# A gate panel ahead of the wait at two stage borders, and the split of the mixed sum in the last step of the last branch

## The reference, cut to what matters

```python
def _merge(att, conv, dn, gz, w_br, w_out):
    gates = jax.nn.sigmoid(gz)
    m = (gates[..., :D_MODEL] * (att @ w_br[0])
         + gates[..., D_MODEL:2 * D_MODEL] * (conv @ w_br[1])
         + gates[..., 2 * D_MODEL:] * (dn @ w_br[2]))
    return m @ w_out

def _token_mixer(u, uc, ...):
    pl = _split_cols(u @ w_in + b_in)
    pc = _split_cols(uc @ w_in + b_in)
    ...
    att_l = _attention_blocked(ql, k_all, v_all)
    conv_l = _short_conv(pl, sc_conv)
    dn_l, dn_c = _dn_bidirectional(...)
    out_l = _merge(att_l, conv_l, _dn_output(dn_l, pl[7], dn_norm_g), pl[12], w_br, w_out)
```

## Time and profile before

| | us |
|---|---|
| timed runs, median (three) | 3375.95 (3371.08 to 3377.99) |
| profiled execution | 3370.39 |
| its span | 3368.6 |
| TensorE matmul busy | 3188.0 (95%) |
| VectorE busy | 1731.9 (51%) |
| ScalarE busy | 1409.3 (42%) |
| DMA queue of the weights, share of 16 engines | 31.0% |
| panels' matmuls (line 1598) on the chain that ended last | 67% |

### The profile page before, as it was taken

How to read it: one execution, slowest core, us unless ns; L and a number is a source line. 1 busy time by engine, 2 the same in 40 slices (tenths; PEclk the granted TensorE clock), 3 DMA queues, 4 the chain that set the end, 5 groups by cost and what they waited for, 6 DMA issues and landing times.

```text
span 3368.6 us, 51444 instructions
## 1 busy us (share of the span) xinstructions
PE 3188.0 (95%) x18766; PEld 2650.5 (79%) x18766; DVE 1731.9 (51%) x3150; ACT 1409.3 (42%) x2197; POOL 131.5 (4%) x126
## 2 busy tenths in 40 slices
PE   4999999999989899999999999999899998899898
PEld 2777768888868578877788868787788888699898
DVE  2333357777743833434333343333678775756555
ACT  3222255565534632224322242223655654653544
POOL 0000001010100000000000000000000000000000
PEclk7999999999999999999999999999899999999999
DMA  6534431111122033222432243444211113144454
GB/s 234 175 127 151 153 113 45 50 50 44 54 66 88 14 115 130 99 87 95 168 100 94 94 144 137 162 133 153 73 48 51 61 45 115 60 142 164 152 183 146
DMA packets 101116, 363.43 MB, mean 108 GB/s; under 512 B 11136, under 2 KB 12672, under 8 KB 100864
## 3 DMA queue, kind: packets, MB, share of 16 engines
q1 hardware_dynamic: 98240, 353.02, 31.0%
q10 hardware_dynamic: 2752, 8.72, 0.8%
HBM read 360.58 MB, written 1.11 MB: 107 GB/s over the span
## 4 chain that ended last, share of the span: by engine, by line
PE 84%; DVE 7%; ACT 4%; issue 3%; DMA 1%; POOL 0%; SPq 0%; DVEq 0%; POOLq 0%; ACTq 0%
PE bank L1598 67%; PE bank L1847 3%; PE bank L1845 2%; DVE wlo L989 2%; PE bank L1623 2%; ACT whi L480 1%; PE bank L1898 1%; ACT scr L910 1%; PE bank L1906 1%; DVE h L1056 1%; PE bank L1916 1%; PE bank L1918 1%; PE bank L2051 1%; PE bank L2074 1%; ACT gc_row L893 1%
## 5 line engine op out<-in xcount | busy, mean ns | idle before, releaser
L1598 PE MATMUL bank<-uh,whi 128*128 128x512 f32 (+1 forms) x3008 | 1117.2, 371 | 49.6 <-ACTq L868 17.0
L1598 PE MATMUL bank<-ul,whi 128*128 128x512 f32 (+1 forms) x3008 | 1084.3, 360 | 0.0
L1598 PE MATMUL bank<-uh,wlo 128*128 128x512 f32 (+1 forms) x3008 | 1081.8, 360 | 0.5 <-DVE scr L1346 0.3
L480 ACT ACTIVATE whi<-raw 128x1024 fp32r<-128x1024 f32 x520 | 548.1, 1055 | 1223.1 <-PE bank L1598 1222.7
L989 DVE TENSOR_TENSOR wlo<-raw,whi 128x1024 fp32r<-128x1024 f32 x520 | 642.0, 1235 | 799.1 <-ACT whi L480 797.7
L1598 PEld LDWEIGHTS bank<-uh,whi 128*128 128x128 f32 x3008 | 577.7, 192 | 155.9 <-issue 60.4
L1598 PEld LDWEIGHTS bank<-uh,wlo 128*128 128x128 f32 x3008 | 576.7, 192 | 82.0 <-DVE scr L1346 1.8
L1598 PEld LDWEIGHTS bank<-ul,whi 128*128 128x128 f32 x3008 | 578.4, 192 | 69.9 <-issue 2.2
L1598 PE MATMUL bank<-bh,whi 128*128 128x512 f32 (+1 forms) x1088 | 387.9, 357 | 1.1 <-DVE h L1056 0.8
L1598 PE MATMUL bank<-bl,whi 128*128 128x512 f32 (+1 forms) x1088 | 384.5, 353 | 0.0
L1598 PE MATMUL bank<-bh,wlo 128*128 128x512 f32 (+1 forms) x1088 | 384.4, 353 | 0.0
(11 more groups left out here) (232 smaller groups left out, 3034.3 us busy)
## 6 DMA issues: line engine op xcount, KB each, us to landing
raw<-stream SPq DMA_DIRECT2D x520, 512.0 KB, 3.3
ada_raw<-stream SPq DMA_DIRECT2D x132, 512.0 KB, 5.1
gc_row<-gc_rows ACTq DMA_DIRECT2D x16, 512.0 KB, 3.7
m<-stream SPq DMA_DIRECT2D x8, 512.0 KB, 11.4
scr<-stream SPq DMA_DIRECT2D x4, 512.0 KB, 13.0
h<-h_in SPq DMA_DIRECT2D x1, 2048.0 KB, 17.3
cst<-consts SPq DMA_DIRECT2D x1, 1298.0 KB, 5.6
out<-m SPq DMA_DIRECT2D x8, 128.0 KB, 1.8
```

The lines of the kernel that those rows point to most:

```text
L480: act.activation(whi[:, j, :], raw[:, j, :], ACT.Copy).then_inc(hi_ready, 1)
L1598: last = mm(bank[j][:, c0:T], w(t, a), x[:, t, c0:T], start=n == 0, stop=n == 3 * kts - 1)
```

## The change

Three edits, in both layers:

1. **Attention to branch 1.** The first gate panel of branch 1 is moved into the attention stage: 6 of its 24 matmuls stand before the last `pv`, 18 behind it. `pair_done[0]` is now raised when the sixth tile's low part is done, and the wait for the attention output (`att_low`) stands before panel 1.
2. **Conv to branch 2.** The wait for conv's output stands before panel 1 of branch 2, not before panel 0.
3. **Branch 2 to output.** In the last step of branch 2, VectorE does 7 of the 8 subtractions of the mixed sum (`m_low`) before it waits for the last panel; ScalarE's copies have waits of their own: tiles 0 to 5 for the last panel but one, tiles 6 and 7 for their sums.

TensorE's branch loops start at 1 for all branches; block 0 is written out.

```diff
             def project_out(l):            # ScalarE
-                act.wait_ge(panel_done, 4 * B0)
-                have(act, pair_done[1], G0)
+                act.wait_ge(panel_done, 4 * B0 - 1)
+                have(act, pair_done[1], G0 - 1)
                 for t in range(KT):
+                    if t >= KT - 2:
+                        have(act, pair_done[t % 2], G0)
                     act.activation(uh[:, t, c0:T], m3[:, t, c0:T], ACT.Copy).then_inc(C["mh_ready"], 1)
...
+            def m_low(l, t):               # VectorE
+                c0 = CTX if l == DEPTH - 1 else 0
+                dve.wait_ge(C["mh_ready"], 8 * l + t + 1)
+                dve.tensor_tensor(ul[:, t, c0:T], m3[:, t, c0:T], uh[:, t, c0:T].bitcast(f32), ALU.subtract).then_inc(C["mx_ready"], 1)
...
                         split(B + 1, 2 * k)
+                        if last and k:
+                            for t in range(KT - 1):
+                                m_low(l, t)
                         dve.wait_ge(panel_done, 4 * B + 2 * k + 2)
...
+                        if j == 6:         # VectorE, out_low in attention
+                            dve.wait_ge(A["att_low"], 8 * l + 7)
+                            dve.sem_inc(pair_done[0], 2)
...
-                for k in range(2):
-                    dve.sem_inc(pair_done[k], 2)
+                dve.sem_inc(pair_done[1], 2)
...
-                for t in range(KT):
-                    dve.wait_ge(C["mh_ready"], 8 * l + t + 1)
-                    dve.tensor_tensor(ul[:, t, c0:T], m3[:, t, c0:T], ...)
+                m_low(l, KT - 1)
...
+                else:                      # TensorE, branch
+                    for j in range(4):
+                        if j == 1:
+                            for s, n in ready:
+                                have(pe, s, n)
+                        if (r, j) != (1, 0):
+                            pair_free(G0, j)
+                            panel(B0, j, *((uh, ul) if j % 2 == 0 else (bh, bl)), c0)
-                with pe.Fori(1 if r == 0 else 0, 4) as i:
+                with pe.Fori(1, 4) as i:
...
+                    if n == N:             # TensorE, attention
+                        pair_free(G1, 0)
+                        panel(B1, 0, uh, ul, c0, hi=6)
                     if n:
                         pv(n - 1)
                     if n < N:
                         turn(n)
+                panel(B1, 0, uh, ul, c0, lo=6)
...
-                branch(l, 1, [(pair_done[0], P[("q", l)][1] + 2), (pair_done[1], P[("q", l)][1] + 2)])
+                branch(l, 1, [(A["att_low"], 8 * l + 7)])
```

More of the change, by code:

```diff
@@ L1394, in branch, with step @@
                 g0, rides = P[("rides", l, "br")] if r == 1 else (0, 0)
-                def step(i):
+                def step(i, last=False):
                     B = B0 + i
@@ L1426, in branch @@
                         step(0)
-                    with steps.loop(1 if r == 0 else 0, 4, 0 if r == 0 else 2) as i:
+                    with steps.loop(1 if r == 0 else 0, 3 if r == 2 else 4, 0 if r == 0 else 2) as i:
                         step(i)
+                    if r == 2:
+                        step(3, True)
                 for k in range(2):
@@ L1552, in project_out @@
                 c0 = CTX if l == DEPTH - 1 else 0
-                for t in range(KT):
-                    dve.wait_ge(C["mh_ready"], 8 * l + t + 1)
-                    dve.tensor_tensor(ul[:, t, c0:T], m3[:, t, c0:T], uh[:, t, c0:T].bitcast(f32), ALU.subtract).then_inc(C["mx_ready"], 1)
+                m_low(l, KT - 1)
                 gates(l, 1)
@@ L1969, in branch @@
                 g0, rides = P[("rides", l, "br")] if r == 1 else (0, 0)
-                for s, n in ready:
-                    have(pe, s, n)
+                if r == 0:
+                    for s, n in ready:
+                        have(pe, s, n)
                 if rides:
@@ L1974, in branch @@
                         for j in range(4):
-                            pair_free(G0 + i, j)
-                            panel(B0 + i, j, *((uh, ul) if j % 2 == 0 else (bh, bl)), c0)
+                            if (i, j) == (0, 1):
+                                for s, n in ready:
+                                    have(pe, s, n)
+                            if (i, j) != (0, 0):
+                                pair_free(G0 + i, j)
+                                panel(B0 + i, j, *((uh, ul) if j % 2 == 0 else (bh, bl)), c0)
                             if j % 2 == 0:
@@ L1991, in branch @@
                             qk_swap(10 * l + j // 2, kT[:, j // 2, :])
-                with pe.Fori(1 if r == 0 else 0, 4) as i:
+                else:
+                    for j in range(4):
+                        if j == 1:
+                            for s, n in ready:
+                                have(pe, s, n)
+                        if (r, j) != (1, 0):
+                            pair_free(G0, j)
+                            panel(B0, j, *((uh, ul) if j % 2 == 0 else (bh, bl)), c0)
+                with pe.Fori(1, 4) as i:
                     for j in range(4):
@@ L2076, in pv @@
                     last.then_inc(A["s_pv"], 1)
+                B1, G1 = P[("br", l, 1)]
                 scores(0)
```

## The result

The changed kernel takes 3354.39 us, the median of six runs (3353.69 to 3357.12), against 3374.17 us for the kernel before, six runs as well. The ratio is 0.9944 (95% interval 0.9933 to 0.9955): faster by 0.56%, 15 to 23 us. The profiled execution has a span of 3352.2 us against 3368.6, 16.4 us less. Forecast were 15.6 us. Between the medians it is 19.8 us: the profiled execution of the kernel before (3370.39 us) was shorter than all six of its timed runs, so the traces show a smaller gain than the medians.

What follows compares the result with a forecast made beforehand. TensorE was taken to bound nearly everything, so removing its idle pays. Conv 12.0, attention 4.6 and output 0.3 - 1.3 sum to 15.6 us: 3375.95 - 15.6 = 3360.4 us, range 3351 to 3369.

Steps and rivals of the forecast that it cites:

- What bounds the kernel: Whole kernel: TensorE has 84% of the span, so an edit pays by the idle time it takes out of TensorE.
- Conv to branch 2: Wait moved behind the gate panel: panel 1 starts 6.7 us sooner in layer 0, 5.3 in layer 1, both 12.0 us.
- Attention to branch 1: Gate matmuls around the last pv fill both idle times: 2.4 us in layer 0, 2.2 in layer 1, both 4.6 us.
- Rivals C and D: C: gate panel only moves the wait, gain 0 to 6 us, chance 0.12. D: written-out blocks make it slower, 0.04.
- Branch 2 to output: No copy runs under the last panel, only the order behind it changes: layer 0 gains 0.3 us, layer 1 loses 1.3.
- rival B: Branch 2's end: the mixed sum really is split under the last panel; gain 24.6 us, 3351.4 us; chance 0.04.
- The forecast wait of some 2 us at tile 7: First output panel, both layers: TensorE stands some 2 us before tile 7, which is last in a longer line.
- 0.3 - 1.3: Second output panel's start after branch 2: 0.3 us gained in layer 0, 1.3 us lost in layer 1.
- The sum: All borders: 12.0 + 4.6 + 0.3 - 1.3 = 15.6 us, from the median 3375.95 to 3360.4 us.
- The clock: Output stage: full speed behind the new idles; slow starts of 1.5 us (layer 0) and 2.4 (layer 1) kept for the range.

Runs made afterwards that it cites:

- the kernel kept warm through the wait: Kernel before, with 18 (layer 0) or 30 (layer 1) matmuls of no use put into the wait behind conv: ratio 0.9993.
- split under the panel: Changed kernel, with ScalarE copying tiles 0 to 6 before slot 3's whi copy and VectorE subtracting tile 7 before the last wlo split: 3348.19 us.

## Why the prediction held, and where it did not

- **What bounds the kernel.** Held: only idle time of TensorE, and its slow matmuls behind it, moved.
- **Conv to branch 2.** Held, 12.3 us for 12.0, and no wait took the place of the old one in layer 0. In layer 1 the two idles were 0.3 and 0.8 us for 0.4 and 1.3. That part of this sum is the slow start was read from the spacing of the matmuls; the kernel kept warm through the wait shows it by itself, 3.8 us. These are distances in traces; edit 2 alone gained 8.9 us between medians, 6 to 13 by its interval.
- **Attention to branch 1.** Held, 4.8 us for 4.6, with both parts of the mechanism: the six before `pv` are worth 0.8 and 0.7 us, and bank 0 was free in time. Timed alone, edit 1 gained 1.1 us.
- **Rivals C and D.** No step was late, and written-out code costs nothing within 0.1%.
- **Branch 2 to output.** The order of the work held. ScalarE's order kept the split from running under the last panel (rival B did not happen, and the kernel that moves ScalarE's copies shows that the order alone was the reason). In layer 0 tile 7 decides, and the mark came 0.7 us earlier for 0.3; in layer 1 0.9 us later for 1.3, and that passed through to the stage's last product (28.62 us behind branch 2's last matmul for 27.71), as forecast. The forecast wait of some 2 us at tile 7 came only where the panel ran at full speed (1.56 us with edit 3 alone); in the changed kernel it was 0.17 us in layer 0.
- **The value of edit 3.** This is the term that failed: "0.3 - 1.3", 1.0 us lost. Beside edits 1 and 2, on one chip, edit 3 gained 3.8 us. The term was worked out against rows in which layer 1's output panel ran at full speed after 2.83 us of idle. Of six kernels without edit 3, all with 2.83 us of idle there, two had full speed behind it (before, and the one with block 0 written out: 6.3 us), and four did not (7.8 to 8.7 us), among them edits 1 and 2. In layer 0 the same six have the mark anywhere from 9.85 to 12.38 us. With edit 3 it is at 10.5 and 7.2 us in all four traces that have the change's order on ScalarE and VectorE, whether the panel starts fast or slowly. So edit 3 gains where the border would have had a long slow start, and loses 0.7 and 0.9 us where it would have had none. Of the 3.8 us the borders explain 2.4; the rest is open.
- **The sum.** It came out near by some luck. The forecast has 16.6 us for edits 1 and 2 and a loss of 1.0 for edit 3. Between medians, edits 1 and 2 gave 13.3 and 14.5 us in two comparisons, and edit 3 another 3.8, so an optimistic and a pessimistic term cancel in part (the first within its interval). Nor do the edits add up: alone they gave 1.1, 8.9 and 0.2 us, 10.2 in sum, against 18.3 and 19.8 for all three. Slow starts at the idles that a single edit leaves account for part of this in the traces; the rest stays open.
- **The clock.** I took full speed behind the new idles, with the slow starts in the range. In the changed kernel it was slow in layer 0 (first matmul 0.76 us) and from the ninth matmul on in layer 1, and it cost next to nothing, since the wait at tile 7 became shorter by as much (0.17 us for 1.56). The slow start was priced about right (1.4 us here for 1.5) and put in the wrong place: what mattered was which of the old ones would go. The 1.39 us of the earlier trace rows, which I took for a short idle followed by a low clock, did not stand alone: TensorE had stood 1.92 and 0.62 us in the six microseconds before, waiting for loads. The Trainium skill says ("TensorE: Matmul & The Clock Gate", section "A second HAM failure mode: psum-queue depth-cycling") that frequent short idles between groups of matmuls make the clock swing between its levels. The rows agree with it only in part: idles of 2.5 and 2.0 us were followed by slow matmuls in the changed kernel, and by full speed up to tile 7 with edit 3 alone. The 1.68 us at attention were followed by full speed in the kernel before (first matmul 0.47 us), but not with block 0 written out (0.77 us).

## What to carry to other kernels

To move work under a panel it is not enough to loosen a wait: follow the engine's own order upwards from the moved instruction, and look whether something ahead of it waits for that very panel. Where work on the busiest engine stands behind a wait that it does not need, move it ahead of the wait: it pays twice, for the idle and for the slow matmuls after it. And don't take a stretch behind an idle of 2 to 4 us from one trace as its price; the same idle was followed by either clock level in neighbouring kernels, and runs of one kernel differ by several microseconds.

## What the runs showed of the hardware that was not expected

- The same idle is followed by either clock level. 2.83 us before layer 1's output panel: granted clock 1.00 over seven microseconds in the kernel before, 0.53 with edits 1 and 2. 3.66 us before layer 0's: full speed with edit 2 alone, slow matmuls in the other five kernels without edit 3.
- Whether the kernel or the execution decides is open. Two profiled executions of edits 1 and 2 agree to 0.02 us in both layers' marks, two of the changed kernel to 0.04, though in the latter the fall in layer 1 comes at the ninth matmul once and at the seventh once. But timed runs of one kernel differ: of the fifteen of the kernel before that ran beside "split under the panel", the six with a mean granted clock of 0.979 to 0.982 took 3370.25 to 3372.95 us and the nine with 0.977 or 0.978 took 3374.10 to 3377.34. On the chip of the single edits the two don't go together so clearly.
- The fall can come during the work and not right after the idle: in the changed kernel layer 1's first eight output matmuls run 0.12 us apart and the next twelve or so 0.21.
- 18 or 30 matmuls whose result nobody reads, put into a wait, made the kernel before no slower (ratio 0.9993, 0.9983 to 1.0002) and panel 1 of its branch 2 begin 1.5 and 2.3 us sooner.
